# Where activations begin within 512 bytes, against the weights, in five up-like phases of a float32 block

## The reference

```python
def swiglu_ffn(x, w_in, w_out):
    gate, up = jnp.split(x @ w_in, 2, axis=-1)
    return (jax.nn.silu(gate) * up) @ w_out

def conv_ffn(x, w_up, conv_w, conv_b, w_down):
    up = x @ w_up
    a, g = up[..., :D_FF_2], up[..., D_FF_2:]
    g = causal_dwconv(g, conv_w) + conv_b
    return (jax.nn.gelu(g) * a) @ w_down

def mixer_c(x, w_in, conv_w, w_out):
    gate_b, gate_c, h = jnp.split(x @ w_in, 3, axis=-1)
    return (gate_b * causal_dwconv(gate_c * h, conv_w)) @ w_out
```

## Time and profile before

| | us |
|---|---|
| three runs | 2281.83, 2287.01, 2291.79 |
| median | 2287.01 |
| profiled execution | 2293.73 |
| its span in the profile | 2291.9 |
| mean granted TensorE clock | 0.998 |

### The profile page before, as it was taken

One profiled execution on the slowest core, in us unless ns is written; L12 is line 12 of the kernel. 1 busy time (PEld: TensorE's weight loads), 2 busy tenths in 40 slices (PEclk: granted clock), 3 DMA queues, 4 the chain that ended last, 5 costly groups with the idle time before them and its releaser, 6 DMA issues.

```text
span 2291.9 us, 35530 instructions
## 1 busy us (share of the span) xinstructions
PE 2274.3 (99%) x15278; PEld 2081.8 (91%) x15278; DVE 1542.2 (67%) x1756; ACT 1019.2 (44%) x1283; POOL 354.9 (15%) x222
## 2 busy tenths in 40 slices
PE   9999999999999999999999999999999999999998
PEld 8999889897799998898988999988998988999987
DVE  7777436564587764356846999835886656999835
ACT  5555335455555543234333555522453442555521
POOL 2332000230133220001000322100230000322100
PEclk9999999999999999999999999999999999999999
DMA  4333323212133332242421333332233522232331
GB/s 171 111 111 111 110 74 139 74 52 78 37 113 109 111 111 102 74 173 90 168 90 37 129 105 112 112 115 77 108 100 124 200 74 74 93 108 99 129 109 55
DMA packets 34732, 238.83 MB, mean 104 GB/s; under 512 B 4108, under 2 KB 4492, under 8 KB 6800
## 3 DMA queue, kind: packets, MB, share of 16 engines
q1 hardware_dynamic: 34432, 236.56, 29.5%
q10 hardware_dynamic: 144, 0.00, 0.0%
HBM read 234.46 MB, written 2.10 MB: 103 GB/s over the span
## 4 chain that ended last, share of the span: by engine, by line
PE 96%; DVE 2%; DMA 1%; POOL 0%; ACT 0%; issue 0%; SPq 0%; DVEq 0%; POOLq 0%
PE bank L646 33%; PE bank L780 30%; PE bank L629 18%; PE bank L745 4%; PE bank L1132 4%; PE bank L768 1%; PE bank L986 1%; PE bank L1160 1%; PE bank L1181 1%; DVE w_lo L1871 1%; DMA raw<-w_full 1%; PE bank L918 0%; PE bank L928 0%; PE bank L825 0%; DVE s_lo L1987 0%
## 5 line engine op out<-in xcount | busy, mean ns | idle before, releaser
L1871 DVE TENSOR_TENSOR w_lo<-raw,w_hi 128x2048 fp32r<-128x2048 f32 (+1 forms) x207 | 475.1, 2296 | 362.5 <-ACT w_hi L1306 313.2
L1306 ACT ACTIVATE w_hi<-raw 128x2048 fp32r<-128x2048 f32 x207 | 395.1, 1909 | 326.0 <-DMA raw<-w_full 319.5
L780 PE MATMUL bank<-w_hi,h_hi 128*128 128x512 f32 x692 | 269.9, 390 | 0.0
L780 PE MATMUL bank<-w_hi,h_lo 128*128 128x512 f32 x692 | 269.4, 389 | 0.0
L780 PE MATMUL bank<-w_lo,h_hi 128*128 128x512 f32 x692 | 269.3, 389 | 0.0
L562 POOL TENSOR_TENSOR s_raw<-raw 128x512 f32<-128x512 f32 x84 | 115.7, 1378 | 545.0 <-PE bank L646 385.4
L646 PE MATMUL bank<-t_hi,s_hi 128*128 128x256 f32 x672 | 187.5, 279 | 3.2 <-ACT cc L1360 3.2
L646 PE MATMUL bank<-t_hi,w_hi 128*128 128x256 f32 x672 | 187.3, 279 | 3.0 <-DVE h L2023 3.0
L646 PE MATMUL bank<-u_hi,w_hi 128*128 128x256 f32 x672 | 187.5, 279 | 0.0
L646 PE MATMUL bank<-u_hi,w_lo 128*128 128x256 f32 x672 | 187.3, 279 | 0.0
L646 PE MATMUL bank<-u_lo,w_hi 128*128 128x256 f32 x672 | 187.2, 279 | 0.0
(11 more groups left out here) (386 smaller groups left out, 6096.9 us busy)
## 6 DMA issues: line engine op xcount, KB each, us to landing
raw<-w_full SPq DMA_DIRECT2D x207, 1024.0 KB, 4.9
rows_ab<-rows SPq DMA_DIRECT2D x8, 1024.0 KB, 7.0
x<-x SPq DMA_DIRECT2D x4, 512.0 KB, 4.5
mem_raw<-mem SPq DMA_DIRECT2D x2, 1024.0 KB, 9.0
out<-x SPq DMA_DIRECT2D x3, 512.0 KB, 2.6
raw<-w_full SPq DMA_DIRECT2D x2, 512.0 KB, 7.3
ab_rows<-ab_rows SPq DMA_DIRECT2D x1, 768.0 KB, 6.4
wg_raw<-w_gates SPq DMA_DIRECT2D x1, 512.0 KB, 7.2
```

Of the source, the lines that this page charges most:

```text
L780: done = mm(bank[:, 2 * t + n, :], act_in[:, k, tok(t)], w[:, s, c0:c0 + T], start=(first and r == 0 and j == 0), stop=(last and r == 1 an ...
L1306: S.activation(w_hi[:, u % SLOTS, :], raw[:, u % SLOTS, :], ACT.Copy).then_inc(w_hi_done, 1)
L1871: V.tensor_tensor(w_lo[:, u % SLOTS, at:FULL], raw[:, u % SLOTS, at:FULL], w_hi[:, u % SLOTS, at:FULL], ALU.subtract).then_inc(w_split, 1)
```

## The change

Tiles are placed otherwise; nothing else is changed in the instructions, their order or their waits. u of up0, up1, cin and up3 becomes a_hi and a_lo (128 within 512, the weights' place) and stays at 320 in up2. T gets two places, t_near at 50 KB (128 within 512) and t_far at 50.1875 KB (320); up0, up2 and cin use the first, up1 and up3 the second.

| phase | u before | T before | u after | T after |
|---|---|---|---|---|
| up0 | 320 | 320 | 128 | 128 |
| up1 | 320 | 320 | 128 | 320 |
| up2 | 320 | 320 | 320 | 128 |
| cin | 320 | 320 | 128 | 128 |
| up3 | 320 | 320 | 128 | 320 |

```diff
-        u_hi = at("u_hi", [P, KD, T], f32r, X0 + 16 * KB + 192)
-        u_lo = at("u_lo", [P, KD, T], f32r, X0 + 32 * KB + 192)
+        u_far = [at(f"u_{n}", [P, KD, T], f32r, X0 + kb * KB + 192) for n, kb in (("hi", 16), ("lo", 32))]
+        u_parts = {0: (a_hi, a_lo), 1: (a_hi, a_lo), 2: u_far, "c": (a_hi, a_lo), 3: (a_hi, a_lo)}
...
-        t_hi = arena("t_hi", [P, 4, KD // 2, T // 2], f32r, 50.1875)
-        t_raw = arena("t_raw", [P, 4, KD // 2, T // 2], f32, 66.1875)
-        t_lo = arena("t_lo", [P, 4, KD // 2, T // 2], f32r, 66.1875)
+        t_near, t_far = ([arena(f"t_{n}{at}", [P, 4, KD // 2, T // 2], dt, at + kb)
+                          for n, dt, kb in (("hi", f32r, 0), ("raw", f32, 16), ("lo", f32r, 16))] for at in (50, 50.1875))
+        t_parts = {0: t_near, 1: t_far, 2: t_near, "c": t_near, 3: t_far}
...
         def high_of(gen):
 
-            return u_hi if gen in UP_GEN.values() else s_hi if gen in ("down0", "down1") else a_hi
+            for f in ORDER:
+                if gen == UP_GEN[f]:
+                    return u_parts[f][0]
+            return s_hi if gen in ("down0", "down1") else a_hi
...
-            def b_block(k, n):
-                return block_b(u_hi, k, n), block_b(u_lo, k, n)
-
-            def t_block(n):
-                return t_hi[:, n - 1, :, :], t_lo[:, n - 1, :, :]
+            def b_block(f, k, n):
+                return block_b(u_parts[f][0], k, n), block_b(u_parts[f][1], k, n)
+
+            def t_block(f, n):
+                return t_parts[f][0][:, n - 1, :, :], t_parts[f][2][:, n - 1, :, :]
```

More of the change, by code:

```diff
@@ L443, in high_of @@
         def high_of(gen):
-            return u_hi if gen in UP_GEN.values() else s_hi if gen in ("down0", "down1") else a_hi
+            for f in ORDER:
+                if gen == UP_GEN[f]:
+                    return u_parts[f][0]
+            return s_hi if gen in ("down0", "down1") else a_hi
         def low_of(gen):
-            return u_lo if gen in UP_GEN.values() else s_lo if gen in ("down0", "down1") else a_lo
+            for f in ORDER:
+                if gen == UP_GEN[f]:
+                    return u_parts[f][1]
+            return s_lo if gen in ("down0", "down1") else a_lo
         def tok(t):
@@ L570, in token_sums @@
                     gp.wait_ge(t_step, 3 * TH[f] + i + 1)
-                    G.tensor_tensor(t_raw[:, n, :, :], t_raw[:, n, :, :], block_b(u_lo, *low), op).then_inc(t_sum, 1)
+                    t_raw = t_parts[f][1]
+                    G.tensor_tensor(t_raw[:, n, :, :], t_raw[:, n, :, :], block_b(u_parts[f][1], *low), op).then_inc(t_sum, 1)
             def up(f):
@@ L612, in parts_of @@
             def parts_of(name):
-                hi, lo = (u_hi, u_lo) if name in NAME.values() else (s_hi, s_lo) if name in ("mixin", "ab") else (a_hi, a_lo)
+                hi, lo = (s_hi, s_lo) if name in ("mixin", "ab") else (a_hi, a_lo)
+                for f in ORDER:
+                    if name == NAME[f]:
+                        hi, lo = u_parts[f]
                 return (w_hi, hi), (w_lo, hi), (w_hi, lo)
@@ L661, in fourth_product @@
                 pe.wait_ge(*c22_at(f, u))
-                product(b, (w_hi[:, s, :], w_lo[:, s, :]), 3 * QS, t_block(4), False).then_inc(gemm_done, 1)
+                product(b, (w_hi[:, s, :], w_lo[:, s, :]), 3 * QS, t_block(f, 4), False).then_inc(gemm_done, 1)
             def seven_unit(f, u):
@@ L678, in seven_unit @@
                     pe.wait_ge(t2_sum, TH[f] + 1)
-                product(b, w, 0, b_block(0, 0), True).then_inc(product_done, 1)
+                product(b, w, 0, b_block(f, 0, 0), True).then_inc(product_done, 1)
                 if split_twice(U0[name] + u):
@@ L683, in seven_unit @@
                     pe.wait_ge(t_split, 4 * TH[f] + 1)
-                product(b + 1, w, 2 * QS, t_block(1), True).then_inc(product_done, 1)
+                product(b + 1, w, 2 * QS, t_block(f, 1), True).then_inc(product_done, 1)
                 if run_starts:
-                    product(b + 2, w, QS, b_block(1, 0), True).then_inc(product_done, 1)
+                    product(b + 2, w, QS, b_block(f, 1, 0), True).then_inc(product_done, 1)
                 else:
@@ L692, in seven_unit @@
                 pe.wait_ge(*copied_at(f, u, "A11 B11"))
-                product(b, s23, 0, t_block(2), False).then_inc(product_done, 1)
+                product(b, s23, 0, t_block(f, 2), False).then_inc(product_done, 1)
                 pe.wait_ge(*copied_at(f, u, "S1 T1"))
-                product(b + 1, s4, 0, b_block(1, 1), False).then_inc(product_done, 1)
+                product(b + 1, s4, 0, b_block(f, 1, 1), False).then_inc(product_done, 1)
                 if not run_starts:
-                    product(b + 2, w, QS, b_block(1, 0), True).then_inc(product_done, 1)
+                    product(b + 2, w, QS, b_block(f, 1, 0), True).then_inc(product_done, 1)
                 if u == FIRST[f]:
@@ L700, in seven_unit @@
                 pe.wait_ge(*copied_at(f, u, "U"))
-                product(b, s23, QS, t_block(3), False).then_inc(gemm_done, 1)
+                product(b, s23, QS, t_block(f, 3), False).then_inc(gemm_done, 1)
             def up_units(f):
@@ L1365, in high_tokens @@
                     act.wait_ge(*((t2_sum, TH[f] + 1) if k == 1 else (t_sum, 3 * TH[f] + (1, None, 2, 3)[k])))
-                    S.activation(t_hi[:, k, :, :], t_raw[:, k, :, :], ACT.Copy).then_inc(t_high, 1)
+                    S.activation(t_parts[f][0][:, k, :, :], t_parts[f][1][:, k, :, :], ACT.Copy).then_inc(t_high, 1)
             def hidden_high(f, u):
@@ L1957, in b @@
                 def b(k, n):
-                    return tiles(block_b(u_hi, k, n)), tiles(block_b(u_lo, k, n))
-                t1, t2, t3, t4 = (tiles(t_raw[:, n, :, :]) for n in range(4))
+                    return tiles(block_b(u_parts[f][0], k, n)), tiles(block_b(u_parts[f][1], k, n))
+                t1, t2, t3, t4 = (tiles(t_parts[f][1][:, n, :, :]) for n in range(4))
                 if which == 1 or which == 3:
@@ L1999, in low_tokens @@
                     dve.wait_ge(t_high, 4 * TH[f] + (1, 3, 2, 4)[k])
-                    V.tensor_tensor(t_lo[:, k, :, :], t_raw[:, k, :, :], t_hi[:, k, :, :], ALU.subtract).then_inc(t_split, 1)
+                    hi, whole, lo = t_parts[f]
+                    V.tensor_tensor(lo[:, k, :, :], whole[:, k, :, :], hi[:, k, :, :], ALU.subtract).then_inc(t_split, 1)
             def hidden_low(f, u):
```

## The result

The changed kernel takes 2305.3 us (median of four runs, 2305.0 to 2306.8); the kernel before took 2286.8 (four runs, 2281.8 to 2291.8). The ratio is 1.0081, 95% interval 1.0055 to 1.0107: slower by 0.8%, where I had forecast 2280 and a range up to 2296. The third rival had said 2307. Its claim on the place, that 256 columns at the weights' own place have one pace and a slow one, is what the trace shows, at another price; its reason, that two reads meet, no run shows. The runs also lie closer together than before: 1.7 us apart instead of 10.

A forecast was written before the change was run, and what follows sets the result against it. TensorE, busy 99% of the span, was taken to bound the kernel through its pace per matmul. From the profiled 2293.7 us: -12.4 - 2.1 - 1.0 + 2.3 = 2280.5, so 2280 us; range 2274 to 2296.

The forecast's parts named there:

- The third rival: up0, cin, T in up2: 256 columns at the weights' place have only the slow pace; +14.0 us, total 2307; chance 0.13.
- Seven-product loops: Line 646, up1 and up3: slow 256-column products become quick, 4.4 ns each; -12.4 us, at worst +14.0.
- Heads: First units of up phases, line 629: 480 slow 256-column matmuls in up0, up1, cin and up3 become quick; -2.1 us.
- 512-column units: 48 matmuls in each of up0, up1, up3 go from 233.3 to 226.7 ns, -1.0 us; cin's 96 counted at nothing.
- Switches: up1, up2, up3: 228 alternations between the two places at 0.01 us each; +2.3 us, bounds 0 and 9.1.
- the first rival: Mixed phases: going from the weights' place to 256 columns at 192 bytes brings the slow pace; total 2289; chance 0.22.
- The spread of the runs: Three runs of the kernel before, fastest 2281.8 us: their differences read as which phases happened to be slow.
- Other engines: DVE's operations on u unchanged; 5% on those on T would be hidden; up3 can hold 113.7 ns as up2 does.
- cin's lowered clock: cin, behind a wait: clock 0.62 on average for 4.5 us could come or go; uncertainty of about 2 us.
- The second rival: Place doesn't matter for 256 columns, a phase's pace is luck; time stays 2287, between 2282 and 2292; chance 0.18.

The follow-up runs named there:

- the small kernel: Kernel of matmuls alone, the whole computation left out, with operand distances and entries varied; no total time given, settled 256-column steps 120.0 ns at 0, 113.3 or 117.8 at 192.

## Why the prediction was wrong

**Seven-product loops, the step that failed.** I took the gain, -12.4 us, "because the nearest row, 512 columns at the same place, holds the quick pace". The widths do not carry over: at distance 0, 512 columns are at 226.7 ns and 256 at 120.0. The term measures +12.5. No row of before had 256 columns at the weights' place, and I let the nearest one decide instead of leaving the sign open. What in the chip makes 256 columns slow there stays open.

**The third rival** had place and sign right; that two reads meet is not shown. Its price was 4.4 ns a matmul, because I gave the unseen case the slower of the two paces that the trace had; it is 6.6. That its total, 2307, came so near 2305 is errors that cancel: up0 cost 9.7 us and not 7.0, up2 5.4 and not 4.0, but up1 and up3 gained 3.7 together where I had them no better than before, and cin paid 1.1 and not 3.0.

**Heads.** -2.1 forecast, and wrong for the same reason: they went to 120.0 as well. up0's piece of 25.33 us became 25.29; with 48 of 512 columns at 226.7 ns, 14.4 are left for 120, 120 ns each (14.1 before), so only the 512 columns paid for it. up3's, at the quick pace before, went from 24.87 to 25.29. up2's went from 24.86 to 25.33 although its u had not moved: it had fallen to the slow pace.

**512-column units.** Right: 226.7 ns each, as said (233 before). In the timeline of up0 after the change:

```profile
43.27 0.39 PE L639 MATMUL bank<-a_hi,w_lo 128*128 128x512 f32 x1
...
43.95 0.39 PE L639 MATMUL bank<-a_hi,w_lo 128*128 128x512 f32 x1
```

Those are three steps in 0.68 us.

**Switches and the first rival.** 2.3 us forecast for 228 switches. Products at 192 in the mixed phases take 114.2 to 114.6 and not 113.3, those at 0 118.9 to 119.2 and not 120.0: 912 x 0.9 ns and 684 x -1.1 ns in up1 cancel, the net is nothing. The first rival's rule, from 0 to 192 always slow, is true of entries from 512 columns (all 33 of the small kernel's were at 117.8) and false of the mixed phases' entries from 256. I had named that difference and still given the rival 0.22.

**The spread of the runs.** Read rightly as the number of slow phases: groups 6 us apart in 23 runs, one slow phase in a profiled execution of 2287.4 us and two in those of 2292.1 and 2293.7, and one group of 2.8 us once the pace is fixed. The changed kernel's small spread is of the same kind: behind unit 2 its products at 192 are entered from 256 columns at 0 over and over.

**Other engines.** Right. GpSimd's sums of T took 2548 ns at the weights' place and 2696 at 192, where they took 2628 before, and neither lengthened a phase; PE was busy for 188.4 of the 188.9 us of up1:

```profile
L578 POOL TENSOR_TENSOR t_raw50.1875_74<-t_raw50.1875_74,a_lo 128x1024 f32<-128x1024 f32 x6 | 16.1, 2696 | 90.7 <-DVE t_raw50.1875_74 L1972 88.4 <-DVE t_raw50.1875_74 L1978 2.3
L578 POOL TENSOR_TENSOR t_raw<-t_raw,a_lo 128x1024 f32<-128x1024 f32 x6 | 15.2, 2548 | 188.7 <-DVE t_raw L1972 184.2 <-DVE t_raw L1978 4.5
```

cin's lowered clock did not come back: the clock is 1.00 over the whole phase after and was 0.98 before.

**The second rival** is out: the pace changes with the distance alone, with no other engine at work, 113.3 to 120.0 ns. The Trainium skill, SBUF — State Buffer, Who interferes with whom, says that PE never waits on anyone. No run here shows PE waiting on another engine's access; what fails is what I drew from the sentence, that the place of TensorE's own operands is nothing to a matmul.

## What to carry to other kernels

A matmul-bound kernel has a pace per matmul; divide the pieces of the chain by their counts and compare phases of the same shape before looking for waits. Where two operands begin matters by their distance and the width, so a row of one width says nothing of another: price a form that the trace does not show from both sides and leave the sign open. If runs fall in groups a fixed step apart, look for a state that persists, and for what hands it on from one phase to the next. Try a remedy from both states: a pair that turns slow into quick also turned quick into slow.

## What the hardware showed beyond what I expected

- 256-column fp32r matmuls in the kernels of matmuls alone: 113.3 ns a step only at exactly 64 or 192 bytes modulo 256 between the operands, and 115.5 to 121.7 at every other distance tried; at 0, 120.0 in all 24 entries of one of them.
- 512 columns: 226.7 ns at 0 and 256, 228.8 or 228.9 at 64 and 320, 231.7 to 234.6 elsewhere.
- At 64 and 192 there are two paces, 113.3 and 117.8. At 192 each lasted for over a thousand matmuls in the whole kernel.
- Two matmuls of 256 columns at distance 0, without a wait, turned the pace at 192 over in 11 of 11 places of the whole kernel. Six or twelve handed over the quick one each time: 18 of 18 in the small kernel, and five phases of the whole one.
